# Gate sums of the second mixer: six levels two at a time, in high and low parts

## The reference

```python
def _mla_gla_mixer(x, w_in, ...):
...
    def log_gate(lr, w2, bias):
        return _heads(jax.nn.log_sigmoid((lr @ w2 + bias).astype(F32)) / GLA_TAU, GLA_HEADS)
    o = _bidirectional_scan(gq_h, _heads(gk, GLA_HEADS), _heads(gv, GLA_HEADS),
                            log_gate(lr_f, gla_w2_f, gla_b_f), log_gate(lr_b, gla_w2_b, gla_b_b))

# what the scan computes, forward (s <= t) and backward (s > t):
# o_t = sum_s (q_t * exp(sum of log_a between s and t)) . k_s v_s^T
```

## Time and profile before

| | us |
|---|---|
| median of 3 runs | 2308.18 |
| lowest, highest | 2307.66, 2313.74 |
| the profiled execution | 2307.74 |
| its span in the profile | 2305.9 |
| TensorE busy | 2157.9 (94%) |
| VectorE busy | 1125.7 (49%) |
| ScalarE busy | 780.0 (34%) |

### The profile page before, as it was taken

The page is one execution under the profiler, slowest core; times in us unless marked ns, Lnnn a source line. Parts: engine busy times, 40 slices in busy tenths (PEclk is TensorE's granted clock), DMA queues, the critical chain, the costliest instruction groups (busy, mean ns, idle before and its releaser), DMA issues.

```text
span 2305.9 us, 30328 instructions
## 1 busy us (share of the span) xinstructions
PE 2157.9 (94%) x12254; PEld 1517.6 (66%) x12254; DVE 1125.7 (49%) x1737; ACT 780.0 (34%) x1295; POOL 62.1 (3%) x62
## 2 busy tenths in 40 slices
PE   8989998798889899988988999999999999989998
PEld 7884443443368844434433688898888888888887
DVE  5682222121156722221211766677666766787666
ACT  3441110111034411101110455454554555554553
POOL 0010000000010100000000000001000000001000
PEclk9999999899999999998999999999999999999999
DMA  9448999999982399999999855533545555534461
GB/s 308 137 183 369 421 421 422 418 421 421 418 263 90 143 370 421 422 421 416 421 421 419 287 175 194 189 129 129 200 165 201 186 179 189 177 107 149 166 212 43
DMA packets 231292, 623.80 MB, mean 271 GB/s; under 512 B 14946, under 2 KB 166564, under 8 KB 181860
## 3 DMA queue, kind: packets, MB, share of 16 engines
q1 hardware_dynamic: 225552, 605.32, 68.8%
q0 software_dynamic: 3040, 10.78, 1.4%
q10 hardware_dynamic: 2548, 5.61, 0.7%
HBM read 620.62 MB, written 1.05 MB: 270 GB/s over the span
## 4 chain that ended last, share of the span: by engine, by line
PE 42%; DMA 5%; DVE 4%; ACT 2%; issue 1%; POOL 0%; SPq 0%; DVEq 0%; ACTq 0%
PE bank_pair L1541 14%; PE bank L1529 10%; PE bank_pair L1542 7%; PE bank L252 4%; PE bank L1369 4%; PE bank_pair L252 2%; DMA ring<-in_ffn_gate 1%; DMA x_tok<-in_moe_w_up 1%; DMA arena<-in_moe_w_up 1%; DMA ring<-in_moe_w_up 1%; DVE w_low L463 1%; PE bank_pair L1698 1%; ACT w_high L456 1%; DVE x_tok L711 0%; DVE x_tok L700 0%
## 5 line engine op out<-in xcount | busy, mean ns | idle before, releaser
L463 DVE TENSOR_TENSOR w_low<-ring,w_high 128x1024 fp32r<-128x1024 f32 x364 | 440.3, 1223 | 268.6 <-ACT w_high L456 268.5
L1541 PE MATMUL bank_pair<-xT_parts,w_high 128*128 128x512 f32 x1408 | 496.2, 396 | 6.0 <-DVE xT_parts L528 6.0
L456 ACT ACTIVATE w_high<-ring 128x1024 fp32r<-128x1024 f32 x364 | 377.4, 1054 | 220.8 <-PE bank_pair L1542 185.9
L1542 PE MATMUL bank_pair<-xT_parts,w_low 128*128 128x256 f32 x1408 | 393.1, 279 | 0.0
L1369 PE MATMUL bank<-ring,arena 128*64 128x512 f32 x1344 | 339.5, 594 | 17.9 <-DMA ring<-in_moe_w_up 5.3
L1541 PEld LDWEIGHTS bank_pair<-xT_parts,w_high 128*128 128x128 f32 x1408 | 264.3, 188 | 70.1 <-DVE xT_parts L528 6.9
L1369 PE MATMUL bank<-w_parts,arena 128*64 128x512 f32 x768 | 260.1, 599 | 13.4 <-DMA w_parts<-in_moe_w_up 6.1
L1542 PEld LDWEIGHTS bank_pair<-xT_parts,w_low 128*128 128x128 f32 x1408 | 265.2, 188 | 3.0
L1369 PEld LDWEIGHTS bank<-ring,arena 128*64 128x64 f32 x1344 | 110.0, 137 | 231.6 <-issue 222.9
L1477 DVE SCALAR_TENSOR_TENSOR arena<-arena,bank 128x512 f32<-128x512 f32 x32 | 23.9, 747 | 436.4 <-PE bank L1369 436.4
L252 PE MATMUL bank<-w_high,xT_parts 128*128 128x256 f32 x1024 | 197.0, 287 | 8.9 <-DVE w_low L463 8.8
(11 more groups left out here) (307 smaller groups left out, 3013.8 us busy)
## 6 DMA issues: line engine op xcount, KB each, us to landing
ring<-in_moe_w_gate SPq DMA_DIRECT2D x56, 1024.0 KB, 23.6
ring<-in_moe_w_up SPq DMA_DIRECT2D x56, 1024.0 KB, 22.6
ring<-in_moe_w_down SPq DMA_DIRECT2D x56, 1024.0 KB, 26.1
ring<-in_ffn_gate SPq DMA_DIRECT2D x44, 1024.0 KB, 6.5
ring<-in_ffn_up SPq DMA_DIRECT2D x44, 1024.0 KB, 5.4
ring<-in_ffn_down SPq DMA_DIRECT2D x44, 1024.0 KB, 6.2
w_parts<-in_moe_w_up SPq DMA_DIRECT2D x32, 1024.0 KB, 25.6
w_parts<-in_moe_w_down SPq DMA_DIRECT2D x32, 1024.0 KB, 26.1
```

Of the source, the lines that this page charges most:

```text
L456: e.activation(hi, src, ACT.Copy).then_inc(*S.high.tell(key))
L463: e.tensor_tensor(lo, src, hi.bitcast(F32), ALU.subtract).then_inc(*S.low.tell(key))
L1541: e.matmul(pairs(bank[:, :]), hi[:, j, :], k.x_parts[:, :, j, :], start=j == 0, stop=False)
L1542: ins = e.matmul(bank[:, 0:T], lo[:, j, :], k.xh[:, j, :], start=False, stop=j == KT - 1)
```

## The change

The six lower levels (6 to 1) of each stream get their sums two levels at a time. `span_two_pe` opens two neighbouring banks, 2 and 3 for the forward stream and 0 and 1 for the backward one, and makes for each of four blocks of gates two fp32r products with 256 columns of a table: the tables of two levels side by side. The two products are the high and the low part of the gates. ScalarE makes the high parts (`la_high`, two copies of 128x512 at the start of `spanned_act`), VectorE the low parts (`la_low`, two subtractions at the start of `spanned_dve`), and ScalarE rounds the table of the six levels once (128x1536, in the step "gates"). Sum 7 of both streams and level 8 stay in fp32. All eight banks are now declared as four pairs.

```diff
 def span_tables():
...
+    ways = ([], [])
     for m in LEVELS:
...
+        ways[0].append(same & np.where(late, (u >= middle) & (u <= t), (u > t) & (u < middle)))
+        ways[1].append(same & np.where(late, (u >= middle) & (u < t), (u >= t) & (u < middle)))
+    out += [ways[0][0], ways[1][0]] + ways[0][1:] + ways[1][1:]
...
     def open_two(self, e, group, key):
-        at = self.turn.get(group, 0)
+        at = self.turn.get(group, 0) if len(group) > 2 else 0
         assert at % 2 == 0
         self.turn[group] = at + 2
-        for side in range(2):
-            i = group[(at + side) % len(group)]
-            old, self.use[i] = self.use[i], key
-            if old is not None and (side == 0 or old != first):
+        self.at[key] = first = group[at % len(group)]
+        for old in dict.fromkeys(self.use[first:first + 2]):
+            if old is not None:
                 e.wait_ge(*self.closed(old))
-            first = old
-        self.at[key] = i - 1
+        self.use[first:first + 2] = [key, key]
...
+def span_two_pe(e, k, d, m):
+
+    S, key = k.S, d.key + ("factor", m - 1)
+    k.banks.open_two(e, O_BANKS if d.forward else A_BANKS, key)
+    e.wait_ge(*S.dve_step["la_low", d.way])
+    e.wait_ge(*S.act_out[("spans_rounded",)])
+    at = LEVELS.index(m) - 1
+    table = k.spans_rounded[:, d.way, at:at + 2, :]
+    for i in range(4):
+        bank = k.bank_tiles[k.banks.at[key] + i // 2]
+        parts = [(part[:, i % 2, block(i // 2)], table) for part in (d.high, d.low)]
+        ins = mm(e, pairs(bank[:, 256 * (i % 2):256 * (i % 2) + 256]), parts)
+    ins.then_inc(*S.product.tell(key))
+
+
 def span_act(e, k, d, m):
     S, key = k.S, d.key + ("factor", m)
-    e.wait_ge(*S.product[key])
+    own = key if m > 6 else d.key + ("factor", m - 1 + m % 2)
+    e.wait_ge(*S.product[own])
     if m < 8:
         e.wait_ge(*S.dve_step[d.key + ("decayed", m + 1)])
-    e.activation(flat(d.factor), k.banks[key][:, :], ACT.Exp, scale=1.0 / GLA_TAU).then_inc(*S.act_out.tell(key))
+    if m > 6:
+        e.activation(flat(d.factor), k.banks[key][:, :], ACT.Exp, scale=1.0 / GLA_TAU).then_inc(*S.act_out.tell(key))
+        return
+    sums = k.bank_pairs[k.banks.at[own] // 2][:, :].rearrange("p (i m t) -> p i m t", i=4, m=2)[:, :, m % 2, :]
+    e.activation(pairs(flat(d.factor), 4), sums, ACT.Exp, scale=1.0 / GLA_TAU).then_inc(*S.act_out.tell(key))
...
     for m in LEVEL_ORDER:
         for d in streams:
-            if m > 1 and not (m == 8 and d.forward):
-                span_pe(e, k, d, m - 1)
+            if m == 8 and not d.forward:
+                span_pe(e, k, d, 7)
+            if m in (7, 5, 3):
+                span_two_pe(e, k, d, m - 1)
             spanned_level_pe(e, k, d, m)
 
 
 def spanned_act(e, k, streams, aside):
+    for d in streams:
+        e.activation(d.high, d.la, ACT.Copy).then_inc(*k.S.act_out.tell(("la_high", d.way)))
...
 def spanned_dve(e, k, streams):
+    S = k.S
+    for d in streams:
+        e.wait_ge(*S.act_out["la_high", d.way])
+        e.tensor_tensor(d.low, d.la, d.high.bitcast(F32), ALU.subtract).then_inc(*S.dve_step.tell(("la_low", d.way)))
     decayed_diagonal_dve(e, k, streams[0])
...
+    highs = [A.take_rounded(2, T), k.rot_rounded[:, :, :]]
...
-    e.dma_start(flat(k.spans[:, :, :, :].rearrange("p m w t -> p (m w) t")), k.A["spans"][:, 3 * P:]).then_inc(*S.wide_loaded.land("spans"))
+    e.dma_start(k.spans_all, k.A["spans"][:, 3 * P:]).then_inc(*S.wide_loaded.land("spans"))
...
         elif what == "gates":
+            e.wait_ge(*S.wide_loaded["spans"])
+            e.activation(k.spans_tile[:, :], k.spans_raw, ACT.Copy).then_inc(*S.act_out.tell(("spans_rounded",)))
...
-    k.bank_tiles = [ctx.enter_context(nc.psum_tensor(f"bank{i}", [P, BANK], F32))[:, :] for i in range(4)]
-    k.bank_pairs = [ctx.enter_context(nc.psum_tensor(f"bank_pair{i}", [P, 2 * BANK], F32)) for i in range(2)]
-    k.bank_tiles += [pair[:, BANK * j:BANK * (j + 1)] for pair in k.bank_pairs for j in range(2)]
+    k.bank_pairs = [ctx.enter_context(nc.psum_tensor(f"bank_pair{i}", [P, 2 * BANK], F32)) for i in range(4)]
+    k.bank_tiles = [pair[:, BANK * j:BANK * (j + 1)] for pair in k.bank_pairs for j in range(2)]
```

More of the change, by code:

```diff
@@ L138, in span_tables @@
         same, late = u // n == t // n, t >= middle
-        out.append(same & np.where(late, (u >= middle) & (u <= t), (u > t) & (u < middle)))
-        out.append(same & np.where(late, (u >= middle) & (u < t), (u >= t) & (u < middle)))
+        ways[0].append(same & np.where(late, (u >= middle) & (u <= t), (u > t) & (u < middle)))
+        ways[1].append(same & np.where(late, (u >= middle) & (u < t), (u >= t) & (u < middle)))
+    out += [ways[0][0], ways[1][0]] + ways[0][1:] + ways[1][1:]
     return np.stack(out, axis=1).astype(np.float32)
@@ L1846, with __init__ @@
 class Spanned:
-    def __init__(self, way, la, q, k, early, rows_of, diag, cross, arena, factor, decayed, spans):
+    def __init__(self, way, la, high, low, q, k, early, rows_of, diag, cross, arena, factor, decayed, spans):
+        self.high, self.low = high, low
         self.key, self.way, self.la, self.q, self.k = ("gla", way), way, la, q, k
@@ L1906, in spanned_copies_dve @@
     where = d.diag.rearrange("p s a (b h x) -> p (s a) b h x", h=2, x=half)[:, :, :, 1 if d.forward else 0, :]
-    scores = k.bank_pairs[k.banks.at[d.last(m)] // 2 - 2][:, :].rearrange("p (a c) -> p a c", a=8)[:, :, 0:P // 2]
+    scores = k.bank_pairs[k.banks.at[d.last(m)] // 2][:, :].rearrange("p (a c) -> p a c", a=8)[:, :, 0:P // 2]
     e.wait_ge(*S.dve_out.now())
@@ L1915, in spanned_cross_act @@
     e.wait_ge(*S.product[d.last(8)])
-    scores = pairs(k.bank_pairs[k.banks.at[d.last(8)] // 2 - 2][:, :])[:, :, 0:2 * P]
+    scores = pairs(k.bank_pairs[k.banks.at[d.last(8)] // 2][:, :])[:, :, 0:2 * P]
     e.activation(d.cross.rearrange("p s i x -> p s (i x)"), scores, ACT.Copy).then_inc(*S.act_out.tell(d.last(8)))
@@ L2075, in od_tiles @@
     crosses = [A.take(2, 2, P) for _ in range(2)]
+    highs = [A.take_rounded(2, T), k.rot_rounded[:, :, :]]
+    assert A.at <= after
     A.at = after
@@ L2083, in od_tiles @@
     for way in range(2):
-        spans = {m: (k.spans[:, LEVELS.index(m), way, :],) * NB for m in LEVELS}
-        spans[8] = end_spans[way]
-        b.streams.append(Spanned(way, b.la[way], b.gq, b.gk, b.gq_at + (2 * T if way == 0 else 0), lambda side, i: (slice(64 * side, 64 * side + 64), i),
+        spans = {8: end_spans[way], 7: (k.spans[:, way, :],) * NB}
+        b.streams.append(Spanned(way, b.la[way], highs[way], pairs(k.gates_low[:, way, 0:2 * T]), b.gq, b.gk, b.gq_at + (2 * T if way == 0 else 0), lambda side, i: (slice(64 * side, 64 * side + 64), i),
                                  b.diag, crosses[way], A.tile, factors[way], decayed[way], spans))
@@ L2658, in tiles_and_signals @@
     k.x_tok, k.acc = sb("x_tok", [P, NB, D]), sb("acc", [P, NB, D])
+    k.gates_low = nc.alloc_sbuf_tensor_at("gates_low", [P, NB, D], F32R, offset=nc.sbuf_base - 4 * NB * D)
     k.mixT = sb("mixT", [P, KT, T])
@@ L2673, in tiles_and_signals @@
     k.rot_tmp = sb("rot_tmp", [P, 2 * T])
+    k.rot_rounded = nc.alloc_sbuf_tensor_at("rot_tmp_rounded", [P, NB, T], F32R, offset=nc.sbuf_base - 8 * T)
     k.junk = k.acc[:, 0, 512:512 + T]
@@ L2692, in tiles_and_signals @@
     k.pool_or_distance = sb("wide_tables", [P, NB * 4 * T])
+    wide_at = nc.sbuf_base - 4 * NB * 4 * T
     k.x_tok_high = nc.alloc_sbuf_tensor_at("x_tok_high", [P, NB, KT, P], F32R, offset=nc.sbuf_base - 4 * NB * D)
@@ L2698, in tiles_and_signals @@
     k.gla_w2 = k.pool_or_distance[:, 2 * P * len(LEVELS):]
-    k.spans = k.pool_or_distance[:, 0:2 * P * len(LEVELS)].rearrange("p (m w t) -> p m w t", w=2, t=P)
+    k.spans_all = k.pool_or_distance[:, 0:2 * P * len(LEVELS)]
+    k.spans = pairs(k.spans_all[:, 0:2 * P])
+    k.spans_raw = k.spans_all[:, 2 * P:]
+    k.spans_tile = nc.alloc_sbuf_tensor_at("spans_rounded", [P, 2 * P * (len(LEVELS) - 1)], F32R, offset=wide_at + 8 * P)
+    k.spans_rounded = k.spans_tile[:, :].rearrange("p (w m t) -> p w m t", w=2, t=P)
     words = nc.sbuf_bytes_remaining // 4 // 8 * 8 - 8
```

## The result

The changed kernel is slower by a little: median 2317.11 us of 16 runs (2306.78 to 2320.02) against 2311.37 us of 16 runs of the kernel before on the same chips (2307.66 to 2313.79). The ratio is 1.0023, with a 95% interval of 1.0015 to 1.0031. The forecast was 2304.1 us, in a range that ended at 2307.3: wrong in its sign, and the range missed the time by 9.8 us.

A forecast was written before the change was run, and what follows sets the result against it. TensorE was taken to set the pace in the second mixer, whose gain passes on to the end. From the profiled 2307.74 us, minus 4.2 for the scan, plus 0.6 for the clock, came 2304.1 us; range 2301.8 to 2307.3.

The forecast's parts named there:

- wait ahead of B6: TensorE idles before the backward stream's level-6 scores until VectorE's copy is done: 0.55 us, once for every two levels.
- scores F8 to F2: Second mixer's scan, forward stream's scores from level 8 to level 2; F2 was expected at about 753.4 instead of 757.77 us.
- scores F8 to values: Second mixer's scan, from the forward stream's level-8 scores to the values, which were expected near 761.9 us.
- the walk: New order of the scan followed with measured durations: multiply F1 (forward, level 1) at 754.8 instead of 759.00, gain 4.2 us.
- Rival (1): In the two-level sums all eight products take a first one's 0.22 us; gain gone, 2307.7 to 2308.3 us; chance 0.04.
- Rival (4): In the expert stage the weight stream sets the pace, so the mixer's gain is lost: 2307.7 us; chance 0.04.
- Rivals (2): At the scan's end the clock falls before F1 and lasts into the values, costing 2.5 us: 2306.0 us; chance 0.15.
- (5): Sums cheaper by 0.6 us in all and no clock fall at the scan's end, 1.45 more: 2301.5 us; chance 0.11.
- the clock term: TensorE's clock at the scan's end, from B2 into the values: between -1.45 and +2.5 us, taken as +0.6.
- rival (3): Inside the scan three 0.55 us gaps each drop the clock for 2.90 us, 1.45 lost each: 2309.0 us; chance 0.04.

The follow-up runs named there:

- e7: Changed kernel plus five unread fp32r products ahead of scores B6, B4 and B2, filling TensorE's waits: median 2308.08 us, ratio 0.9985 to the kernel before.
- e6: e2 plus unread fp32r products ahead of scores F1 (7), B1 (6) and the values (12): median 2305.82 us, ratio 0.9979 to the kernel before.
- e9: e7 plus unread fp32r products ahead of scores F1 (5), B1 (5) and the values (12): median 2306.33 us, ratio 0.9970 to the kernel before.
- e10: Kernel before plus four fp32 filler products ahead of scores B1 and six ahead of the values: median 2311.91 us, ratio 1.0002 to the kernel before.
- e8: The changed kernel run again unaltered, on the chip of e5 and e7: median 2314.45 us, ratio 1.0007 to the kernel before.
- e5: e2 plus one VectorE addition of 128x1024 between multiply B6 and copy B7, putting a wait back: median 2309.44 us, ratio 0.9991 to the kernel before.
- e2: Changed kernel with sums (4,3) and (2,1) moved behind their stream's even scores, same work: median 2306.73 us, ratio 0.9983 to the kernel before.
- e1: Changed kernel with fp32 two-level sums, without high and low parts or rounded table: median 2310.80 us, ratio 1.0005 to the kernel before.
- e3: Changed kernel with eight more overwritten fp32r products ahead of each two-level sum, waits left: median 2315.36 us, ratio 1.0015 to the kernel before.
- e4: Kernel before with high and low parts in fp32r, one level at a time, order and banks kept: median 2311.98 us, ratio 1.0003.

## Why the prediction was wrong

| step | forecast | measured |
|---|---|---|
| a two-level sum | 1.06 us | 1.13 |
| wait ahead of B6 | 0.55 | 0.61 |
| rounding of the table, hidden | 1.5 | 1.47, hidden |
| high parts, each, hidden | 0.6 | 0.66, hidden |
| low parts, from start to start, hidden | 0.61 | 0.61 (0.69 each), hidden |
| scores F8 to F2, clock at 1.00 | 20.5 | 20.9 (e7) |
| scores F8 to values, clock at 1.00 | 29.0 | 29.7 (e7) |
| loss to the clock, F8 to values | 0 | 8.2 (after against e7, single traces) |

**Right were the walk and what was costed at nothing.** The rows of after for the rounding of the table, for a high and a low part and for the multiply F7:

```profile
710.92 1.47 ACT L2247 ACTIVATE spans_rounded<-wide_tables 128x1536 fp32r<-128x1536 f32 x1
713.56 1.23 ACT L2250 ACTIVATE mixT<-mixT 128x512 f32<-128x512 f32 x2 [1.17 <-DVE mixT L2052]
...
733.39 0.66 ACT L1956 ACTIVATE arena_rounded<-mixT 128x512 fp32r<-128x512 f32 x1
...
734.08 0.69 DVE L1971 TENSOR_TENSOR gates_low<-mixT,arena_rounded 128x512 fp32r<-128x512 f32 x1
...
737.55 0.69 DVE L1766 TENSOR_TENSOR arena<-arena 128x512 f32<-128x512 f32 x1 [0.75 <-PE bank_pair L1913]
```

ScalarE still waits 1.17 us for VectorE behind the rounding, as it waited 2.54 before, and the multiply F7 still waits 0.75 us for its scores: nothing of that came onto the path. e7 gives the walk in full. With the clock held over the scan and lost in the tail, as the sum had it, the change brings 33.17 - 29.70 = 3.5 us of scan and 3.1 us at the median; 3.6 was forecast. Rival (1), the pace of a first product, is out: 0.12 us each. Rival (4) is out: what the scan gains or loses stood at SyncE's first load as well: from the values to it, it is 13.6 to 14.0 us in every trace but those of e6, e9 and e10, where the clock behind the scan changed too (12.2). It also stood at the second block, whose first product comes 5.0 us later after F8 in after than before, and 5.3 earlier in e7. Rivals (2) and (5) spoke of the tail only: in e7 the clock was low from 763 to 770, over the scores B1 (1.80 us instead of 1.11) and into the values (5.52 instead of 5.20), about 1.0 us more than before where +0.6 was taken. They did not decide the result.

**The step that failed is the clock term**, "+0.6" between -1.45 and +2.5, and in rival (3) the price and with it the chance. The term looked for idle time at the end of the scan alone. Rival (3) named the right mechanism, the right place and even the right sign, and was given 0.04. It went wrong twice. It took a fall to last as long as the one of the trace of before, 2.90 us, so that three would be needed to turn the gain into a loss. One is enough: it lasted 34 us in the traces of after and e8 and 24 in e5. The values came 37.90 us after F8 instead of the 29.0 walked; 0.7 of these 8.9 us stand in e7 as well, the other 8.2 are the clock's. And it argued that TensorE is busy over 90% of a period, whereas the row of the fall had 1.11 busy us of 3.90. That row bounded nothing from above: in 740 to 746 TensorE was busy 5.39 of 6.00 us, and the clock fell. In the trace of before the scan up to the scores B2 has no idle time at all, 25.62 busy of 25.70, and so held nothing that could be read for a wait of 0.6 us there; the honest bound was the clock at 0.50 to the end of the mixer. Further on it does hold single waits: TensorE idles 1.04 us ahead of B1 and 0.65 us ahead of 778.13, and the clock is still 1.00 right behind either. They show that one wait may pass, and nothing of what a fall costs:

```profile
778.13 0.63 PE L751 MATMUL bank_pair<-tables,acc 128*128 128x128 f32 x4 [0.65 <-DVE acc L2009]
```

The section "A second HAM failure mode: psum-queue depth-cycling" of the Trainium skill's "TensorE: Matmul & The Clock Gate", which the prediction named for rival (3), says that short idle times between groups of products make the clock swing. The traces agree that they make it fall; here, once fallen, it did not swing back but stayed for 34 us.

**What is shown and what is not.** Shown is that the waits bring the loss: filled, with all else unchanged, the clock holds and 6.4 us come back (e7 against e8). Shown is that the same sums without waits don't bring it (e7, and e2 up to its first wait), and that the fall can come with fp32 sums too (e1). Shown is also that a single wait may pass: the first one was followed by the fall in two traces (after, e8), the second in three (e1, e3, e5), and neither in two (e2, e6). That some runs of the changed kernel have no fall at all rests on their times and mean clocks. In e1 and e3, whose sums are longer, the clock came back within about 3.5 us; in after, e5 and e8 it did not for 24 to 34 us, although TensorE was busy nearly throughout. There it came back within the values, 32 fp32 products in a row, as it did in each of the nine traces in which it was low when they began, 2.9 to 5.8 us after their start. That longer groups of products are what brings it back fits all of this, but wasn't tried by itself: what of the work counts (length of the sums, their share beside the scores of 64 rows) stays open. So does why the same program falls in one run and not in the next.

## What to carry to other kernels

When a change makes one engine's work shorter than that of the engine that feeds it, the slack can come back as short waits, as here, and on TensorE such a wait may cost the clock as well as itself: take as the upper bound half clock up to the next long group of products, not the length of the wait. Fill the wait, with work that is due anyway (e2) or with products that nobody reads (e7, e9), and look at the granted clock stretch by stretch. A profiled execution can lie some microseconds from the median; the sum should start from the median of many runs, and times inside a trace be taken from a mark just ahead of the change.

## What the runs showed of the hardware

- With TensorE busy nearly all the time, on sums of eight fp32r products and scores of 64 rows and 64 columns, the granted clock stayed at 0.50 for 24 to 34 us (e5; after and e8). At that clock an fp32r product of 256 columns takes 0.21 us instead of 0.12, and 16 score records 1.97 instead of 1.11.
- An fp32r product of 128 columns (e4) takes about as long as one of 256 (after): 0.11 to 0.12 us from start to start. The fp32r products of 256 columns were 0.12 us apart, not the 0.109 that the prediction cited as an estimate from the Trainium skill ("TensorE: Matmul & The Clock Gate", "Back-to-back issue gap").
- One and the same program takes 2305.94 to 2318.81 us (e8), with the mean clock of a run going from 0.986 to 0.978. The scan is 8 to 9 us longer in the traces with the fall (37.90 and 38.4) than in that of e7 (29.70), so whether the clock falls is probably most of the spread.
